# One hybrid decoder layer on one core: read the half blocks ahead of the weight casts, move two DVE products behind the start of T, and regroup the tail of the last pass

## The reference

```
h = rmsnorm(x); proj = h @ w_in      # q|k|v, beta/decay logits, z, two GLU halves, gate_a, gate_b
q, k, v = silu(conv4(...)); q, k l2-normed
a = strict(beta * (k k^T) * decay);  T = (I + a)^-1        # per head and chunk
u = T (beta v - ...), o = q S + (q k^T * decay) u,  S' = g S + k^T u    # chunk after chunk
o_A = rmsnorm(o) * silu(z)
o_B = silu(layernorm(conv31(glu)))
mixed = sigmoid(gate_a) * o_A + sigmoid(gate_b) * o_B
x = x + rmsnorm(mixed @ w_out);  y = x + rmsnorm(relu(rmsnorm(x) @ w_up)^2 @ w_down)
```

## Time and profile before

| | |
|---|---|
| median of 3 runs | 1156.14 us (1155.63 to 1156.26) |
| the profiled execution | 1156.82 us, its span 1154.7 us |
| PE busy | 1109.1 us, 96% of the span |
| DVE, ACT, POOL busy | 727.0, 523.8, 583.6 us |
| passes 1 to 7 | from about 92 us to 589 us, 70.97 us for one turn of the loop |
| last pass | about 574 us to 679 us |
| output projection, then FFN | from 679 us to the end |

### The profile page before, as it was taken

The page is one execution under the profiler, slowest core; times in us unless marked ns, Lnnn a source line. Parts: engine busy times, 40 slices in busy tenths (PEclk is TensorE's granted clock), DMA queues, the critical chain, the costliest instruction groups (busy, mean ns, idle before and its releaser), DMA issues.

```text
span 1154.7 us, 22229 instructions
## 1 busy us (share of the span) xinstructions
PE 1109.1 (96%) x8311; PEld 1073.4 (93%) x8311; DVE 727.0 (63%) x1141; ACT 523.8 (45%) x939; POOL 583.6 (51%) x512
## 2 busy tenths in 40 slices
PE   6789999999999999999999989999999999999996
PEld 5589989999899999999989889999999999999996
DVE  5669897887979879798775357662144125314735
ACT  5554545545555454555555665442133123214441
POOL 0327548476583855748575464133333333335831
PEclk9889999999999999999999999999999999999999
DMA  6121222212231122311222124122322222222302
GB/s 237 37 86 37 84 78 89 74 36 85 74 101 58 36 85 74 101 58 53 89 92 56 55 76 174 56 74 75 90 77 89 77 88 78 85 79 86 108 21 82
DMA packets 32519, 92.12 MB, mean 80 GB/s; under 512 B 4688, under 2 KB 12240, under 8 KB 32464
## 3 DMA queue, kind: packets, MB, share of 16 engines
q1 hardware_dynamic: 32464, 91.35, 25.0%
HBM read 82.82 MB, written 8.52 MB: 79 GB/s over the span
## 4 chain that ended last, share of the span: by engine, by line
PE 81%; ACT 7%; DVE 6%; issue 5%; DMA 0%; POOL 0%; ACTq 0%; DVEq 0%; SPq 0%
PE ps L572 29%; PE ps L601 27%; PE ps L610 6%; PE ps L935 4%; DVE ps L1398 2%; DVE work L1395 2%; PE ps L768 2%; PE ps L821 1%; PE ps L740 1%; PE ps L758 1%; ACT w_hi L1015 1%; PE ps L633 1%; PE ps L620 1%; DVE o_a L1398 1%; ACT L1005 1%
## 5 line engine op out<-in xcount | busy, mean ns | idle before, releaser
L1891 POOL TENSOR_TENSOR w_lo<-raw,w_hi 128x1024 fp32r<-128x1024 f32 x123 | 298.6, 2429 | 382.6 <-ACT w_hi L1033 225.8
L601 PE MATMUL ps<-in_hi,w_hi 128*128 128x288 f32 x992 | 307.0, 310 | 5.1 <-ACT work L1114 2.6
L601 PE MATMUL ps<-in_hi,w_lo 128*128 128x288 f32 x992 | 302.1, 305 | 0.0
L601 PE MATMUL ps<-in_lo,w_hi 128*128 128x288 f32 x992 | 300.4, 303 | 0.0
L601 PEld LDWEIGHTS ps<-in_hi,w_hi 128*128 128x128 f32 x992 | 190.3, 192 | 8.9 <-ACT work L1114 4.2
L601 PEld LDWEIGHTS ps<-in_hi,w_lo 128*128 128x128 f32 x992 | 190.3, 192 | 1.5
L601 PEld LDWEIGHTS ps<-in_lo,w_hi 128*128 128x128 f32 x992 | 190.2, 192 | 0.7
L1398 DVE SCALAR_TENSOR_TENSOR ps<-work,ct,ps 128x512 f32<-128x512 f32 x240 | 180.6, 752 | 7.4 <-DVE work L1521 1.7
L1033 ACT CAST w_hi<-raw 128x1024 fp32r<-128x1024 f32 x61 | 63.8, 1048 | 224.2 <-PE ps L572 224.2
L1395 DVE TENSOR_TENSOR f_tmp<-f_tmp 128x576 f32<-128x576 f32 x31 | 70.7, 2280 | 96.4 <-ACT f_tmp L1345 91.0
L1395 DVE TENSOR_TENSOR o_a<-o_a,ps 128x576 f32<-128x576 f32 (+1 forms) x40 | 25.3, 634 | 144.7 <-PE ps L572 122.8
(11 more groups left out here) (309 smaller groups left out, 2283.8 us busy)
## 6 DMA issues: line engine op xcount, KB each, us to landing
raw<-w_all_in SPq DMA_DIRECT2D x136, 512.0 KB, 3.6
work<-s_in_in SPq DMA_DIRECT2D x8, 512.0 KB, 3.3
s_sample_out<-work SPq DMA_DIRECT2D x8, 512.0 KB, 2.7
xt<-x_t_in SPq DMA_DIRECT2D x4, 576.0 KB, 6.4
xt<-x_t_in SPq DMA_DIRECT2D x2, 1152.0 KB, 7.1
y_out<-o_a SPq DMA_DIRECT2D x16, 144.0 KB, 1.7
halo<-halos_in SPq DMA_DIRECT2D x9, 156.0 KB, 3.5
conf_rows_out<-c_rows SPq DMA_DIRECT2D x8, 135.0 KB, 2.1
```

Of the source, the lines that this page charges most:

```text
L601: t = mm(dense_ps(n, j, h), a[:, w, k], b[:, k, h * HALF:(h + 1) * HALF], start=r == 0, stop=r == PASS_MM // 2 - 1)
L1891: return gp.tensor_tensor(out, a, b, op)
```

## The change

1. In passes 1 to 8 ACT reads both half blocks of a step before it casts (before: casts first). Pass 0 is as it was.
2. DVE at step 5: T (prompt and samples) is made right behind `t0_ps` and ahead of the two `qk` products. The samples' T lies in `hms` now; the samples' `db` is gone: `at` of the samples is one scalar_tensor_tensor of `dm`, beta and the PSUM product. PE waits for `qk_ready` at step 9. `k_tr` and `v_tr` become one semaphore.
3. POOL in the last pass: the first U is made at step 5, ahead of step 6's `w_lo`. DVE makes the samples' sums at steps 3 and 6 (before 5 and 8) and the taps at 1, 2, 6, 8 (before 1, 2, 3, 6).
4. ACT at the end of the last pass: chunk 2's u and the samples' u go ahead of the second four Silus, job 7's two half blocks are read behind them, the output casts 0 and 1 stand at step 24 and cast 2 at step 28.
5. `gate_b`: DVE multiplies blocks 0 to 6 itself, just ahead of its sums, at steps 25, 26, 27, 29, 30; POOL keeps the two halves of block 7.

```diff
@@ tensor, steps 2, 8, 9
-                        nc.tensor.transpose(g(2)[0:SMP, 0:P], sm(v["kn"], P), con("ident")).then_inc(k_tr, 1)
-                        nc.tensor.transpose(g(3)[0:SMP, 0:P], sm(v["vc"], P), con("ident")).then_inc(v_tr, 1)
+                        nc.tensor.transpose(g(2)[0:SMP, 0:P], sm(v["kn"], P), con("ident")).then_inc(kv_tr, 1)
+                        nc.tensor.transpose(g(3)[0:SMP, 0:P], sm(v["vc"], P), con("ident")).then_inc(kv_tr, 1)
...
-                            r = mm(g(2)[0:SMP, 0:SMP], c_s[(l - 1) % 2], sma("dm"), start=True, stop=True)
+                            r = mm(g(2)[0:SMP, 0:SMP], c_s[(l - 1) % 2], v["hms"], start=True, stop=True)
...
                             pe.wait_ge(u0_ready, n)
+                            pe.wait_ge(qk_ready, n)
@@ splits, last pass
-            if last(n) and s in (24, 25, 26):
-                out.append((8, ("out", s - 24)))
+            if last(n) and s in (24, 28):
+                out += [(8, ("out", off)) for off in ((0, 1) if s == 24 else (2,))]
@@ scalar, phase
                 for s in range(33):
-                    for m, off in splits(n, s):
-                        if isinstance(off, tuple):
-                            split(8, off[1])
-                        else:
-                            proj_split(m, off)
+                    if first(n):
+                        casts(n, s)
                     pos, j = evac_first(n, s)
-                    if pos is not None:
+                    if pos is not None and not (last(n) and pos == 7):
...
-                    if pos is not None and not (first(n) and j == CB) and not (last(n) and pos == 9):
+                    if pos is not None and not (first(n) and j == CB) and not (last(n) and pos in (7, 9)):
                         act.wait_ge(job_done, 2 * (base(n) + pos) + 2)
                         half_read(n, pos, j, 1)
+                    if not first(n):
+                        casts(n, s)
...
                     if s in (22, 24, 26, 28):
-                        c = (s - 22) // 2
-                        act.wait_ge(u_ps, TILES * n - 3 + c)
-                        A(tile(v["u"], c), g(1)[:, 0:P], ACT.Copy,
-                          scale=hc[:, 5 * BETA + c:5 * BETA + c + 1]).then_inc(u_ready, 1)
+                        chunk_u(n, (s - 22) // 2)
+                    if s == 26:
+                        samples_u(n)
                     if last(n) and s in (24, 26):
...
-                    if s == 26:
-                        act.wait_ge(us_ps, n)
-                        A(smw(v["u"]), g(1)[0:SMP, P:2 * P], ACT.Copy,
-                          scale=hc[0:SMP, 5 * BETA + 4:5 * BETA + 5]).then_inc(us_ready, 1)
+                    if last(n) and s == 26:
+                        for h in range(2):
+                            act.wait_ge(job_done, 2 * (base(n) + 7) + 1 + h)
+                            half_read(n, 7, GB, h)
@@ vector, head
-                    tt(pr(v["db"]), pr(v["dm"]), hcol(BETA), ALU.mult)
-                    tt(sm(v["db"]), sm(v["dm"]), hcol_s(BETA, SMP), ALU.mult).then_inc(db_ready, 1)
+                    tt(pr(v["db"]), pr(v["dm"]), hcol(BETA), ALU.mult).then_inc(db_ready, 1)
...
-                    tt(sm(v["at"]), g(2)[0:SMP, 0:SMP], sm(v["db"]), ALU.mult).then_inc(at_ready, 1)
+                    stt(sm(v["at"]), sm(v["dm"]), hc[0:SMP, 5 * BETA + 4:5 * BETA + 5], g(2)[0:SMP, 0:SMP],
+                        ALU.mult, ALU.mult).then_inc(at_ready, 1)
...
                     tt(g4(0), g4(0), pr(v["u"]), ALU.mult).then_inc(t0_ps, 1)
+                    dve.wait_ge(t0_ps, n)
+                    tt(v["hms"][0:SMP], con("ident", SMP)[:, 0:SMP], g(2)[0:SMP, 0:SMP], ALU.add)
+                    tt(pr(t_r), idents(), g4(0), ALU.add).then_inc(t_ready, 1)
                     dve.wait_ge(qk_ps, n)
                     tt(v["qk"][:, 0:SEQ], g(1), v["dm"][:, 0:SEQ], ALU.mult)
                     tt(sm(v["qk"]), g(3)[0:SMP, 0:SMP], sm(v["dm"]), ALU.mult).then_inc(qk_ready, 1)
-                    dve.wait_ge(t0_ps, n)
-                    tt(pr(t_r), idents(), g4(0), ALU.add)
-                    dve.wait_ge(qk_ready, n)
-                    tt(sm(v["dm"]), con("ident", SMP)[:, 0:SMP], g(2)[0:SMP, 0:SMP], ALU.add).then_inc(t_ready, 1)
@@ vector, convolutions and last pass
-            early_8 = {1: 3, 2: 2, 3: 2, 6: 2}
+            early_8 = {1: 3, 2: 2, 6: 2, 8: 2}
-                samples = (5, 8) if last(n) else (14, 18)
+                samples = (3, 6) if last(n) else (14, 18)
...
-                    if last(n) and 28 <= s < 32:
-
-                        for k in {28: (0, 1), 29: (2, 3, 4), 30: (5,), 31: (6,)}[s]:
+                    if last(n) and s in (25, 26, 27, 29, 30):
+
+                        ks = {25: (0, 1), 26: (2,), 27: (3, 4), 29: (5,), 30: (6,)}[s]
+                        for k in ks:
+                            dve.wait_ge(b_silu, k + 1)
+                            dve.wait_ge(act_read, 2 * (base(H) + 2 + k) + 2)
+                            tt(conf[:, k], conf[:, k], gate[:, k], ALU.mult).then_inc(b_gated, 1)
+                        for k in ks:
                             dve.wait_ge(b_gated, k + 1)
                             tt(conf[:, k], conf[:, k], o_a[:, k], ALU.add).then_inc(mixed, 1)
@@ gpsimd
                         tt(c_s[0][0:SMP], sm(v["at"]), lvl_s(1), ALU.mult).then_inc(c1_ready, 1)
-                    if s == 6:
-
                         pool.wait_ge(c1_ready, n)
                         tt(pr2(uc_r), ident2(), pr2(c_r[0].bitcast(F32)), ALU.subtract)
                         tt(v["us"][0:SMP], con("ident", SMP)[:, 0:SMP], c_s[0][0:SMP], ALU.subtract).then_inc(u0_ready, 1)
+                    if s == 6:
                         pool.wait_ge(qk_ps, n)
...
-                    if last(n) and s in (25, 26, 27, 28, 30):
-
-                        for k in {25: (0, 1, 2), 26: (3,), 27: (4,), 28: (5,), 30: (6,)}[s]:
-                            gate_b(k)
                     if last(n) and s == 31:
-                        gate_b(7, 0)
+                        gate_b(0)
```

More of the change, by code:

```diff
@@ L317, in build @@
         conv4_prod = sem("conv4_prod")
-        k_tr, v_tr, gk_ready, vt_ready = sem("k_tr"), sem("v_tr"), sem("gk_ready"), sem("vt_ready")
+        kv_tr, gk_ready, vt_ready = sem("kv_tr"), sem("gk_ready"), sem("vt_ready")
         gam_ps, kk_ps, qk_ps = sem("gam_ps"), sem("kk_ps"), sem("qk_ps")
@@ L433, in build @@
         c1_ready = sem("c1_ready")
+        b_gated_p = sem("b_gated_p")
         next_exp, next_ready, hm_ready, t0_ps = sem("next_exp"), sem("next_ready"), sem("hm_ready"), sem("t0_ps")
@@ L1116, in half_read, with casts, chunk_u, samples_u @@
                           ACT.Copy).then_inc(act_read, 1)
+            def casts(n, s):
+                for m, off in splits(n, s):
+                    if isinstance(off, tuple):
+                        split(8, off[1])
+                    else:
+                        proj_split(m, off)
+            def chunk_u(n, c):
+                act.wait_ge(u_ps, TILES * n - 3 + c)
+                A(tile(v["u"], c), g(1)[:, 0:P], ACT.Copy,
+                  scale=hc[:, 5 * BETA + c:5 * BETA + c + 1]).then_inc(u_ready, 1)
+            def samples_u(n):
+                act.wait_ge(us_ps, n)
+                A(smw(v["u"]), g(1)[0:SMP, P:2 * P], ACT.Copy,
+                  scale=hc[0:SMP, 5 * BETA + 4:5 * BETA + 5]).then_inc(us_ready, 1)
             def phase(n):
@@ L1185, in phase @@
                     if s == 2:
-                        act.wait_ge(v_tr, n)
+                        act.wait_ge(kv_tr, 2 * n)
                         A(v["vt"][:, 0:SEQ], g(1), ACT.Copy)
@@ L1432, in _ @@
             dve.wait_ge(pads_ready, 1)
-            for ap in (sma("dm"), sma("qk"), wide("u", SEQ), v["us"], v["cs0"], v["cs1"], v["gks"]):
+            for ap in (sma("dm"), sma("qk"), wide("u", SEQ), v["us"], v["cs0"], v["cs1"], v["gks"], v["hms"]):
                 ve.memset(padding(ap), 0.0)
@@ L1544, in head @@
                 if s == 2:
-                    dve.wait_ge(k_tr, n)
+                    dve.wait_ge(kv_tr, 2 * n - 1)
                     dve.wait_ge(hc_ready, n)
@@ L1596, in head @@
                         if l < LEVELS_S:
-                            r = tt(sm(v["dm"]), sm(v["dm"]), g(2)[0:SMP, 0:SMP], ALU.subtract)
+                            r = tt(v["hms"][0:SMP], v["hms"][0:SMP], g(2)[0:SMP, 0:SMP], ALU.subtract)
                         r.then_inc(t_ready, 1)
@@ L1751, in last_head @@
                 dve.wait_ge(head_out, H + 1 + h)
-                dve.wait_ge(b_gated, KB + h)
+                dve.wait_ge(b_gated_p, 1 + h)
                 c_ = half_of(conf[:, KB - 1], h)
@@ L1901, in split, with gate_b @@
                 tt(lo, raw[:, (off + 2) % RING], hi.bitcast(F32), ALU.subtract).then_inc(w_low, 1)
-            def gate_b(k, h=None):
+            def gate_b(h):
+                k = KB - 1
                 pool.wait_ge(b_silu, k + 1)
```

(8 more changed lines are left out.)

## The result

| | before | after |
|---|---|---|
| median, 4 runs each | 1155.89 us (1155.15 to 1156.26) | 1137.39 us (1135.92 to 1137.87) |
| profiled execution, its span | 1156.82, 1154.7 us | 1137.24, 1135.2 us |
| one turn of the loop | 70.97 us | 69.95 us |
| saved up to the last pass | | 7.5 us |
| saved in the last pass | | 12.0 us |

The ratio is 0.9839, with a 95% interval of 0.9822 to 0.9856: 18.5 us by the medians, 19.6 by the two profiled executions. The forecast was 15.0 us, and the lower end of its range, 1139.4 us, lies 2.0 us above the median.

The account below looks back on a forecast made before the run. PE, busy 96% of the span, was taken as the bound, so edits were worth its waits and slow clock: 4.4 + 4.2 + 5.6 - 0.2 + 1.2 - 0.2 = 15.0 us, 1156.1 to 1141.1 us, range 1139.4 to 1145.6.

Parts of the forecast that it names:

- the term of passes 1 to 8: Thirteen PE waits at L1114 and L740, for half block reads and T: 4.4 us saved, bounds 4.2 to 5.0.
- the copy held: DVE's copy of taps before T stands still behind POOL's w_lo, so T gains nothing more: lower bound, 4.2 us.
- ACT's order: End of last pass, waits at L809 and L788: 1.7 and 2.5 us plus 1.4 of slow clock, 5.6 us saved.
- L610: Two waits in the last pass, 1.4 us, go with seven gates on DVE: 1.2 us taken, bounds 0.4 to 1.4.
- chunk 3's u: End of last pass: becomes the next late input, u at 664.7 against PE's arrival at 665.2; 0.2 us lost.
- the state update: Last pass: chunk 2's or 3's may be held behind a gate, costing PE up to 0.7 us; 0.2 taken.
- the first U: Last pass, wait at L758: 2.6 us and 1.7 of slow clock go; 4.2 us counted, bounds 2.5 to 4.3.
- the 13 waits: Passes 1 to 8, PE's list: 2.6 us at L1114 and 2.4 at L740; all gone gives the 5.0 us bound.
- the reordering: Passes 1 to 8: T ahead of q's products comes 0.7 to 0.8 us earlier, just covering the needed 0.6.
- the third rival: More than counted: copy gets through, chunk 3's u in time, L610 clean; 1.2 us more, 1139.6 us; chance 0.13.
- The delayed cast: Passes 1 to 8: ACT's cast ends 0.37 us later behind the reads; costed at nothing, covered by slack.
- The slack of the block at 390.5: POOL's w_lo ends at 389.53, PE begins at 390.5: 1.0 us, of which the first two edits take 0.6.

Follow-up runs that it names:

- c1: The changed kernel with T made five times in a row, four times for nothing: 1148.34 us, ratio 0.9935.
- a3: The changed kernel with the samples' 64 x 64 db product put back behind the large one: 1142.44 us, ratio 0.9897.
- a2: The kernel before with T ahead of q's products and no db product for the samples, casts still ahead of the reads: 1153.98 us, ratio 0.9990.
- a1: The kernel before with only the half blocks' reads put ahead of the casts: 1159.32 us, ratio 1.0039.
- d1: The kernel before with parts 1 and 2 of the change together, the last pass as it was: 1153.46 us, ratio 0.9971.
- b4: The changed kernel with the seven gates back on POOL at their old steps: 1142.66 us, ratio 0.9884.
- b2: The changed kernel with the last pass's first U behind step 6's w_lo again, samples' sums at steps 5 and 8: 1141.71 us, ratio 0.9872.
- b3: The changed kernel with ACT's order near the end as it was before, gates still on DVE: 1143.22 us, ratio 0.9888.
- a4: The changed kernel with q's two products ahead of T again, the db product still gone: 1136.22 us, ratio 0.9838.
- c2: The changed kernel with the half blocks' reads ahead of the casts in pass 0 as well: 1135.05 us, ratio 0.9819.
- c3: The changed kernel with pass 0's reads first too, and its late job's first half block read in ACT's idle time inside the logits: 1133.45 us, ratio 0.9806.

## Why the prediction fell short

The direction and the places in the last pass were right. What failed is the term of passes 1 to 8, in its unit and in the case that I took for the likeliest, the copy held. By the starts the terms are off by 3.1 us there, 0.5 for ACT's order, 0.7 for L610, 0.2 each for chunk 3's u and the state update, and -0.2 for the first U: 15.0 + 4.5 = 19.5 us, what the two profiled executions show; the medians show 1 us less.

- **Passes 1 to 8, 4.4 us: the mis-sized term, measured 7.5.** Two errors lie in it. The first is the unit: I took the 13 waits from PE's list, 2.6 + 2.4 = 5.0 us, and called that the upper bound. By the starts the same thirteen are worth 7.6 (the first of them by its end alone, since it is still there), and c1 shows a listed wait lacking 0.15 to 0.20 us where nothing else is changed. The second is a step that would have gone the other way: "the copy held, near the first bound". Had it been held, the turn would be a3's 70.80 us or a2's 70.71, no more than 0.26 us better than before, and not the 70.4 I derived. I had set the 0.7 to 0.8 us of the reordering against 0.6 to be covered; by the starts it was 0.55 for the old wait, 0.5 for PE's earlier arrival, and the later `w_lo` on top. The gain is there because the copy gets through, which I had put into the third rival and priced at 0.6 us in all. It gets through by 4 to 9 ns in the kernel after; nobody had aimed at that, so this part of the gain is luck.
- **The delayed cast "at nothing".** It was not nothing but half of the mechanism. The cast that ends 0.37 us later starts `w_lo` later (5.80 us of idle in POOL instead of 5.45), and the product that is gone brings the copy 0.13 us ahead: only with both does the copy start first. a1 and a2 have one each, and the copy takes 2.33 and 2.35 us in both; d1 has both, and the turn is 69.96. I had costed the two edits as two waits, each by itself. My own rows had it: `w_lo` at 375.96 and 0.37 later is 376.33, and the copy would have taken the place of the product at 376.30. The slack of the block at 390.5, for which I had looked, never came into play.
- **The rule of the Trainium skill** ("SBUF — State Buffer", the section "Who interferes with whom"), that the second of two such instructions stands still until the first ends, agrees with the rows of the copy, 0.16 or 2.33 us, and of the product, 0.21 or 2.12. In b4 the sum of 10.17 us stood still for longer than any one of POOL's instructions. I used it to decide that the copy is held. It asks which of the two starts first, and that was a matter of 0.3 us which I did not work out.
- **The first U, 4.2 us:** 4.3 by the starts, less 0.3 at L739; b2 gives 4.3. Right.
- **ACT's order, 5.6 us:** 6.1 by the starts, b3 gives 5.8. Right but for the unit: its two waits are 0.15 to 0.2 us each above the list. Chunk 3's u, 0.2 us, was in time: it started at 652.78 and PE came at 653.22 without a wait.
- **L610, 1.2 us:** 1.9, and no state update was held (0.2). In DVE's rows after, three gates and a sum take longer than 0.75 us (1.69, 1.77, 1.36 and 1.59), each beside an instruction of POOL's, 3.4 us in all; I had allowed 4.2 us for it. But b4 shows the term to be another thing than I thought: with ACT's new order the gates' move saves 5.3 us, since POOL's gates would then meet DVE's sums ahead of a state update.
- **From the waits to the sum.** Six lines of 13.2 us in the list are 16.5 us by the starts; 3.0 us of slow clock and 0.3 of single slow steps behind waits are saved as well, and 0.3 are lost at L739: the 19.5 us by which the starts differ in the end. The range had its lower end at "1.2 us more than I count"; the error of the unit, 3 us, was in none of its bounds.

## What to carry to other kernels

Size a wait of a pipelined engine by the distance between the starts before and behind it, less the usual one; the idle time that a list gives is too small by the overlap of each entry, and with many short waits that is a large part. Where one engine's instruction stands still beside another's, as the copy and `w_lo` do here, work out which starts first and by how much, and treat everything that shifts either start, a deleted product or a cast that ends later, as part of one edit. Take a change apart before you trust its parts: here one half alone made the kernel slower, the other did nothing that could be measured, and together they gave the loop 1.02 us per turn.

## What the hardware showed that I had not expected

A DVE addition of two SBUF tiles stood still for 10.17 us (b4) while POOL went through seven instructions in a row: it was not let in between them. And a start decides it sharply: in the kernel after, the copy and `w_lo` begin both at 371.85 us, the copy 4 ns ahead, and it takes 0.16; 0.12 us behind the start of `w_lo` (a3) it takes 2.33. In the traces of a4, b2, b3, b4, c1, c2, c3 and d1 the copy is ahead by 1 to 17 ns in every one of the seven passes, and never held.
